# Two operand tiles swap roles behind a hybrid mixer, and four head groups are split beside the last projections

## The chip, the cores and the metric

The kernel runs on one core of one Trainium2 chip. The metric is the device time of one execution in microseconds, smaller is better. All 256 tokens of one sequence go through two transformer blocks in a single launch, everything in fp32. The large products use split operands: each fp32 matrix is written as hi + lo, both in the matmul format fp32r, and each product is the sum of hi·hi, lo·hi and hi·lo.

## The reference, cut to what matters

The model width is 2048. The first block is a conformer convolution and an MLP. The second block, in which the change lies, is

```python
x = x + hybrid_mixer(x, ...)      # below
x = x + cross_attention(x, mem, ...)
x = x + conv_ffn(x, ...)
return rmsnorm_2(x, final_norm_g)

def hybrid_mixer(x, ...):
    h = rmsnorm_2(x, norm_g)
    proj = h @ w_in                       # q, k, v, z (1024 each), b, a, then q, k, v of moba
    ...
    o_a = gated_delta_rule(l2norm(q_a), l2norm(k_a), v_a, g, beta)
    o_a = rmsnorm_2(o_a, gdn_norm_g) * silu(z_a)     # 8 heads of 128
    o_b = rmsnorm_2(moba_attention(q_b, k_b, v_b, rel_bias), moba_norm_g)   # 8 heads of 128
    return concatenate([o_a, o_b]) @ w_out           # 2048 x 2048
```

## The kernel before

**Weights.** Every weight matrix comes in slots of 512 KB. For a slot i, SP loads `w_raw`, ACT writes `w_hi` (L461), and DVE (L468) or POOL (L476), every other slot in the mixer, writes `w_lo`. Each of the three buffers is a ring of four. ACT makes `w_hi` of slot i+4 only when TensorE has used slot i.

**Order.** Every engine's program is written out by hand in the same order of slots. After each slot an engine calls `step()`, which advances the generators that are registered as work "beside" by one `yield` each. `finish()` steps until they are all over. An engine works strictly in its program's order, so a beside instruction that waits holds up the slots behind it.

**The mixer.** Counting slots from the mixer's first: six products `w_in` of 8 slots (1 to 48), six `moba` products (49 to 96), then z: `("w_in", 3, 0)` is slots 97 to 104 and `("w_in", 3, 1)` slots 105 to 112. Then comes `w_out`, eight pieces of 4 slots, 113 to 144, in `W_OUT_ORDER` = (1,0), (1,1), (0,0), (0,1), (1,2), (0,2), (1,3), (0,3). Half 1 contracts over the moba heads (parts 2 and 3 of the operand), half 0 over the delta-rule heads (parts 0 and 1); a part is four heads, 128 x 1024 values. Beside the slots runs `side_work`: both delta groups, moba heads 0 to 3, `norm(0)`, from step 98 on moba heads 4 to 7, `norm(1)` and, last, `gated(0)`. A moba head takes scores (L2061), bias and maximum on DVE (L2117 to L2124), exp on ACT (L2089), a turn by transposes (L2069), its copy on ACT (L2093), and the product with v (L2076). `norm(g)` scales rows on DVE (L2159), turns them on TensorE (L2031) and copies them back with a gain on ACT (L2038). `gated(g)` multiplies the delta output with silu(z) on DVE (L2372), then also L2031 and L2038. silu(z) is `z_block` (L2272), which reads the accumulator of `("w_in", 3, g)`.

**Operands.** `k.h` (`h_operand`, hi and lo, 16 tiles of 256 tokens) is the input of every `w_in` and `moba` product. The mixer's output is split into the same `k.h`, by `act_part` (hi, L649) and `dve_part` (lo, L655), so ACT first waits for the last `w_in` product:

```python
k.act_beside.finish()
act.wait_ge(*k.pe_done.at("w_in", 3, 1))
for g in range(2):
    act_part(k, act, k.h, 2 + g, CT, k.mk[g], k.act_done.at("moba norm", g), "heads_out")
```

TensorE runs `finish()`, in which the turn of `gated(0)` falls, between slot 112 and slot 113. `k.mid` (`mid_operand`) is the input of `xq` and of the FFN's gate and up products, and `k.h` then holds the cross-attention output and the FFN's hidden chunks. `k.mid` is allocated over the mixer's own work tiles, which are free by the time it is first written.

Of the kernel before, what the change touches and what calls it, by code (L numbers as in the profile page):

```python
# [229 lines left out]
class Kernel:  # L230
# [34 lines left out]
    def buffers(self):  # L265
# [38 lines left out]
        with ExitStack() as second:  # L304
            sb = lambda name, shape, dt=F32: self.sbuf(name, shape, dt, second)
            self.dt_bias, self.a_log = sb("dt_bias", [P, NG]), sb("a_log", [P, NG])
            self.beta, self.g, self.cum, self.grown, self.k_decay, self.beta_unit, self.beta_decay, self.half_log = (
                sb(n, [P, TT, NG]) for n in ("beta", "log_decay", "cum", "grown", "k_decay", "beta_unit", "beta_decay", "half_log"))
            self.logs, self.unit, self.o_small = (sb(n, [P, 2, TT, NG]) for n in ("logs", "unit", "o_small"))
            self.small = sb("gate_small", [P, 3, TT, NG])  # L310
            self.ba, self.token_col = sb("ba", [P, TT, 2 * NG]), sb("token_column", [P, TT])
            self.ba_rows = sb("ba_rows", [2 * NG, T])
            self.w_ba = sb("w_ba", [P, KT * 2 * NG])
            self.w_ba_hi, self.w_ba_lo = (sb(n, [P, KT * 2 * NG + P - 2 * NG], F32R) for n in ("w_ba_hi", "w_ba_lo"))
            self.work = sb("delta_work", [P, 5, TT, CT, P])
            self.state, self.ends = sb("state", [P, CT, HD]), sb("last_decay", [P, TT, 2, NG])
            self.pad = sb("conv_pad", [P, CT, GDN_K - 1 + T])
            self.v_own = sb("moba_v", [P, TT, NM * HD])
            self.moba_small, self.moba_root = sb("moba_small", [P, NM, 3, TT]), sb("moba_root", [P, NM, TT])
        self.mid = side_by_side(self.sbuf("mid_operand", [P, KT, 2, T], F32R))  # L320
# [1816 lines left out]
def act_moba_norm(k, act, g):  # L2137
    root = k.moba_root[:, g * CT:(g + 1) * CT, :]
    act.wait_ge(*k.dve_done.at("moba sums", g))
    act.activation(root, root, ACT.Ln, scale=1.0 / HD).then_inc(*k.act_done.mark())  # L2140
    act.wait_ge(*k.act_done.last())
    act.activation(root, root, ACT.Exp, scale=-0.5).then_inc(*k.act_done.mark("moba roots", g))
    yield
    act_turned(k, act, "moba norm", g, k.mk[g], "moba_norm_g_2")
    yield


def dve_moba_norm(k, dve, g):
# [12 lines left out]
    yield  # L2161

# [16 lines left out]

def side_work(delta, head, norm, gated):  # L2180
    steps = 0
# [13 lines left out]
    yield from counted(norm(1))  # L2195
    yield from counted(gated(0))


def pe_mixer(k, pe):
# [17 lines left out]
    k.pe_beside.start(after(3, pe_two_norms(k, pe)))  # L2217
    k.pe_beside.start(side_work(lambda g: pe_delta(k, pe, g), lambda h: pe_moba(k, pe, h), lambda g: pe_moba_norm(k, pe, g), gated))
    ready = operand_ready(k, "mix_norm")
# [9 lines left out]
    for g in range(2):  # L2229
        pe_product(k, pe, ("w_in", 3, g), k.h, ready, tokens_out=True)  # L2230
    k.pe_beside.finish()
    k.pe_beside.start(gated(1))
    heads_ready = operand_ready(k, "heads_out")
    for n, (half, b) in enumerate(W_OUT_ORDER):
        pe_product(k, pe, ("w_out", half, b), k.h, heads_ready, k_tiles=range(half * KT // 2, (half + 1) * KT // 2),
                   held=("mixer", b), opening=half == 1, closing=half == 0)


def act_mixer(k, act):
# [60 lines left out]
    k.act_beside.start(side_work(delta, lambda h: act_moba(k, act, h), lambda g: act_moba_norm(k, act, g), gated))  # L2300
    for g in range(2):
# [9 lines left out]
    for g in range(2):  # L2311
        act_product(k, act, ("w_in", 3, g), lambda: z_block(g))
    k.act_beside.finish()
    act.wait_ge(*k.pe_done.at("w_in", 3, 1))
    for g in range(2):
        act_part(k, act, k.h, 2 + g, CT, k.mk[g], k.act_done.at("moba norm", g), "heads_out")

    def first_half():
        yield
        act_part(k, act, k.h, 0, CT, k.z[0], k.act_done.at("gated", 0), "heads_out")  # L2320
        act_turned(k, act, "gated", 1, k.z[1], "gdn_norm_g_2")
        act_part(k, act, k.h, 1, CT, k.z[1], k.act_done.last(), "heads_out")
        yield
    k.act_beside.start(first_half())
    for half, b in W_OUT_ORDER:
        act_product(k, act, ("w_out", half, b),
                    None if half else (lambda: act_next(k, act, "xattn_norm", b, k.mid, None, ("w_out", 0, b), "xattn_norm_g_2")))


def dve_mixer(k, dve):  # L2330
# [39 lines left out]
    def gated(g):  # L2370
        dve.wait_ge(*k.act_done.at("z", g))
        dve.tensor_tensor(k.o[g], k.o[g], k.z_tok[g], ALU.mult).then_inc(*k.dve_done.mark("gated", g))  # L2372
        yield
        yield

    def add(b):
        dve_residual(k, dve, ("w_out", 0, b), b, ("mixer", b), [k.dve_done.at("group", "final1", b)])
        dve_prepare(k, dve, "xattn_norm", b, "xattn_norm_g_2", k.mid)
# [3 lines left out]
    k.dve_beside.start(side_work(lambda g: dve_delta(k, dve, g), lambda h: dve_moba(k, dve, h), lambda g: dve_moba_norm(k, dve, g),  # L2382
                                 gated))
    for g in range(2):
# [14 lines left out]
    def first_half():  # L2399
        yield  # L2400
        dve_part(k, dve, k.h, 0, CT, k.z[0], "heads_out")
        dve_part(k, dve, k.h, 1, CT, k.z[1], "heads_out")
        yield
    k.dve_beside.start(first_half())
    for half, b in W_OUT_ORDER:
# [25 lines left out]
def pe_cross(k, pe):  # L2431
    k.pe_beside.start(after(3, pe_total_beside(k, pe, "xattn_norm")))
    pe_product(k, pe, ("xq",), k.mid, operand_ready(k, "xattn_norm"))
    k.pe_beside.finish()
# [8 lines left out]
    for b in range(CT):  # L2443
        pe_product(k, pe, ("xo", b), k.h, operand_ready(k, "cross_out"), k_tiles=range(NX))


def act_cross(k, act):
# [11 lines left out]
    act.wait_ge(*k.pe_done.at("w_out", 0, CT - 1))  # L2459
    act_part(k, act, k.h, 0, NX, k.cross_o, k.act_done.last(), "cross_out")  # L2460
    for b in range(CT):
        act_product(k, act, ("xo", b), lambda: act_next(k, act, "ffn_norm", b, k.mid, ("xq",), ("xo", b), "ffn_norm_g_2"))


def dve_cross(k, dve):
# [11 lines left out]
    for _ in in_turn([head(h) for h in range(NX)], 3):  # L2477
        pass
    dve_part(k, dve, k.h, 0, NX, k.cross_o, "cross_out")

    def add(b):
        before = [k.act_done.at("squares", "xattn_norm", b)]
        dve_residual(k, dve, ("xo", b), b, ("xo", b), before)
        dve_prepare(k, dve, "ffn_norm", b, "ffn_norm_g_2", k.mid)
        k.dve_beside.start(after(1, dve_squares_of_x(k, dve, "ffn_norm", b)))
# [265 lines left out]
```

## Time and profile before

| | us |
|---|---|
| median of 3 runs | 2533.34 (2531.56 to 2536.05) |
| the profiled execution's own time | 2533.18 |
| its span, first to last instruction | 2531.9 |
| TensorE busy | 2449.0 (97%) |
| DVE / ACT / POOL busy | 1646.3 / 1119.0 / 258.9 |
| mean granted TensorE clock | 0.985 |

The span is what the trace covers, and the own time has 1.3 us around it. Times in the rows below are microseconds from the start of the span. In a timeline, the bracket at the end of a row is how long the engine sat idle before it and who released it. PE is TensorE.

### The profile page before, as it was taken

To read this page: it belongs to the slowest core of one execution; us is meant where nothing else is said; L and a number is where in the kernel's file an instruction comes from. 1 tells how busy PE (TensorE), PEld (TensorE's weight loads), DVE (VectorE), ACT (ScalarE), POOL (GpSimd) and SP (SyncE) were. 2 spreads that over 40 slices of the span, in tenths; PEclk is the share of its full clock that TensorE was granted. 3 is DMA by queue.
4 is the path that set the end of the run, shared out by engine and by line. 5 is a ranking of instruction groups with operands and counts; after the bars stand their busy time and mean duration, and the time that the engine had idled before them with its cause. 6 is when DMAs were issued, how large, how long until landed. Compare 5 with 4: busy or idle time off the path is not lost.

```text
span 2531.9 us, 36755 instructions
## 1 busy us (share of the span) xinstructions
PE 2449.0 (97%) x14956; PEld 2190.6 (87%) x14956; DVE 1646.3 (65%) x2274; ACT 1119.0 (44%) x1477; POOL 258.9 (10%) x129
## 2 busy tenths in 40 slices
PE   8999999999999999989899999897999999999997
PEld 7888698888888888889897998797888888888886
DVE  4999766666666666777646443354776676767677
ACT  4000445544454454455436355454544444444443
POOL 0000000000000000023323333330010000000000
PEclk9999999999999999999999999898999999999998
DMA  7445456665666666555334355352565655565663
GB/s 233 154 142 174 159 190 192 192 188 187 193 188 191 193 191 186 185 159 148 88 105 117 100 153 153 128 177 93 182 190 191 191 190 185 192 190 192 190 190 119
DMA packets 377575, 428.05 MB, mean 169 GB/s; under 512 B 16408, under 2 KB 323904, under 8 KB 377408
## 3 DMA queue, kind: packets, MB, share of 16 engines
q1 hardware_dynamic: 372288, 421.58, 54.0%
q10 hardware_dynamic: 5120, 4.12, 0.5%
q8 instruction: 120, 1.97, 0.3%
q14 instruction: 47, 0.39, 0.0%
HBM read 423.54 MB, written 3.67 MB: 169 GB/s over the span
## 4 chain that ended last, share of the span: by engine, by line
PE 92%; ACT 3%; DVE 3%; issue 1%; DMA 0%; POOL 0%; ACTq 0%; DVEq 0%
PE product L560 37%; PE product L509 19%; PE product L562 19%; PE product L534 10%; PE product L531 1%; ACT w_hi L461 1%; PE small L1675 1%; PE small L1689 1%; PE small L1685 1%; DVE w_lo L468 0%; DVE delta_work L1912 0%; DVE x_residual L617 0%; PE small L896 0%; PE small L1728 0%; DMA masks<-in_masks 0%
## 5 line engine op out<-in xcount | busy, mean ns | idle before, releaser
L468 DVE TENSOR_TENSOR w_lo<-w_raw,w_hi 128x1024 fp32r<-128x1024 f32 x640 | 794.1, 1244 | 533.9 <-ACT w_hi L461 533.1
L461 ACT ACTIVATE w_hi<-w_raw 128x1024 fp32r<-128x1024 f32 x712 | 750.4, 1057 | 861.7 <-PE product L562 568.7
L560 PE MATMUL product<-h_operand,w_hi 128*128 128x512 f32 x1728 | 600.0, 393 | 0.0
L560 PE MATMUL product<-mid_operand,w_hi 128*128 128x512 f32 x1408 | 490.2, 392 | 4.2 <-DVE x_residual L763 4.2
L562 PE MATMUL product<-h_operand,w_lo 128*128 128x256 f32 x1728 | 480.9, 278 | 0.0
L562 PE MATMUL product<-mid_operand,w_lo 128*128 128x256 f32 x1408 | 394.8, 280 | 0.0
L560 PEld LDWEIGHTS product<-h_operand,w_hi 128*128 128x128 f32 x1728 | 323.7, 187 | 73.6
L509 PE MATMUL product<-h_operand,w_hi 128*128 128x256 f32 x1920 | 361.3, 290 | 11.0 <-DVE h_operand L655 6.0
L560 PE MATMUL product<-mlp_hidden,w_hi 128*128 128x512 f32 x1024 | 355.7, 394 | 0.9 <-DVE x_residual L617 0.8
L476 POOL TENSOR_TENSOR w_lo<-w_raw,w_hi 128x1024 fp32r<-128x1024 f32 x72 | 180.7, 2510 | 1448.3 <-ACT w_hi L461 1448.3
L562 PEld LDWEIGHTS product<-h_operand,w_lo 128*128 128x128 f32 x1728 | 325.2, 188 | 0.0
L509 PEld LDWEIGHTS product<-h_operand,w_hi 128*128 128x128 f32 x1920 | 305.8, 196 | 15.5 <-POOL w_lo L476 4.0
L560 PEld LDWEIGHTS product<-mid_operand,w_hi 128*128 128x128 f32 x1408 | 264.1, 188 | 62.5 <-DVE x_residual L763 4.5
L562 PE MATMUL product<-mlp_hidden,w_lo 128*128 128x256 f32 x1024 | 283.7, 277 | 0.0
L509 PE MATMUL product<-h_operand,w_lo 128*128 128x256 f32 x960 | 274.7, 286 | 0.0
L562 PEld LDWEIGHTS product<-mid_operand,w_lo 128*128 128x128 f32 x1408 | 266.8, 189 | 0.0
L534 PE MATMUL product<-h_plain,w_raw 128*128 128x256 f32 x1024 | 224.2, 381 | 10.8 <-ACT h_plain L951 10.8
L560 PEld LDWEIGHTS product<-mlp_hidden,w_hi 128*128 128x128 f32 x1024 | 192.0, 188 | 46.2 <-DVE x_residual L617 1.1
L534 PEld LDWEIGHTS product<-h_plain,w_raw 128*128 128x128 f32 x1024 | 195.4, 191 | 38.1 <-DMA w_raw<-in_cc_w_in 10.8
L562 PEld LDWEIGHTS product<-mlp_hidden,w_lo 128*128 128x128 f32 x1024 | 192.1, 188 | 0.0
L1097 DVE SCALAR_TENSOR_TENSOR conv_out<-glu,feature_columns,conv_out 128x256 f32<-128x256 f32 x480 | 190.9, 478 | 0.0
L509 PEld LDWEIGHTS product<-h_operand,w_lo 128*128 128x128 f32 x960 | 187.5, 195 | 0.0
(291 smaller groups left out, 2277.0 us busy)
## 6 DMA issues: line engine op xcount, KB each, us to landing
w_raw<-in_mlp_w SPq DMA_DIRECT2D x256, 512.0 KB, 3.7
w_raw<-in_w_in SPq DMA_DIRECT2D x112, 512.0 KB, 3.8
w_raw<-in_w_gate SPq DMA_DIRECT2D x88, 512.0 KB, 3.5
w_raw<-in_w_up SPq DMA_DIRECT2D x88, 512.0 KB, 3.8
w_raw<-in_w_down SPq DMA_DIRECT2D x88, 512.0 KB, 3.4
w_raw<-in_cc_w_in SPq DMA_DIRECT2D x128, 256.0 KB, 3.0
w_raw<-in_cc_w_out SPq DMA_DIRECT2D x32, 512.0 KB, 4.6
w_raw<-in_w_out SPq DMA_DIRECT2D x32, 512.0 KB, 4.2
```

Source lines behind the costliest of these rows:

```text
L461: act.activation(k.w_hi[i % SPLIT], k.w_raw[i % RAW], ACT.Copy).then_inc(*k.act_done.mark("w_hi", i))
L468: dve.tensor_tensor(k.w_lo[i % SPLIT], k.w_raw[i % RAW], k.w_hi[i % SPLIT].bitcast(F32), ALU.subtract).then_inc(*k.dve_done.mark("w_lo", i))
L476: pool.tensor_tensor(k.w_lo[i % SPLIT], k.w_raw[i % RAW], k.w_hi[i % SPLIT].bitcast(F32), ALU.subtract).then_inc(*k.pool_done.mark("w_lo", i))
L509: done = pe.matmul(out, stationary, moving, start=first and opens, stop=final, skip_group_check=True)
L531: done = pe.matmul(psum[:, part * COLS:(part + 1) * COLS], x[:, kt, cut(part)], w[:, kk, :], start=first, stop=final, skip_group_check=True)
L534: done = pe.matmul(psum[:, part * T:(part + 1) * T], w[:, kk, cut(part)], x[:, kt, :], start=first and part % 2 == 0, stop=final, skip_gro ...
L560: pe.matmul(out, hi[:, kk, n], x.both[:, kt].rearrange("p a t -> p (a t)"), start=s == 0 and kk == 0, stop=False, skip_group_check=True)
L562: done = pe.matmul(out[:, 0:T], lo[:, kk, n], x.hi[:, kt, :], start=False, stop=last and kk == WIDE_K - 1, skip_group_check=True)
L1097: dve.scalar_tensor_tensor(out=out, in0=tap, scalar=w, in1=out, op0=ALU.mult, op1=ALU.add).then_inc(*k.dve_done.mark("tap", t, b, j))
L1675: done = pe.matmul(bank[:, cut(h)], k.off[t][:, h, :], k.a[t][:, h, :], start=True, stop=True)
L1685: done = pe.matmul(bank[:, cut(h)], u[:, h, :], y[:, h, :], start=True, stop=True)
L1689: done = pe.matmul(bank[:, cut(h)], y[:, h, :], u[:, h, :], start=True, stop=True)
```

## The change

The mixer's output is split into `k.mid` in place of `k.h`. `k.h` becomes the operand that `k.mid` was (input of `xq`, gate and up), and `k.mid` takes over the cross-attention output and the FFN's hidden chunks. The tile `mid_operand` is allocated higher up (a spacer `below_mid`), over the parts of the mixer's work tiles that are free early, and these tiles are reordered. With that, the splits need no longer wait for the last `w_in` product: parts 2 and 3 are split inside `norm(0)` and `norm(1)`, part 0 and part 1 inside `gated(0)` and `gated(1)`. `gated(0)` leaves `side_work` and is started after `("w_in", 3, 0)`, beside `("w_in", 3, 1)`; `gated(1)` is started after the `finish()` behind `("w_in", 3, 1)`.

```diff
+            below_mid = 2 * NG + 8 * TT * NG + 3 * 2 * TT * NG + 3 * TT * NG + TT * 2 * NG + TT + NM * 3 * TT + NM * TT + TT * NM * HD
+            self.work = sb("delta_work", [P, 5, TT, CT, P])
...
+        self.sbuf("below_mid", [P, below_mid + TT * CT * P])
         self.mid = side_by_side(self.sbuf("mid_operand", [P, KT, 2, T], F32R))
...
-        self.ffn_mid = [side_by_side(self.h.both[:, i * CT:(i + 1) * CT]) for i in range(FFN_MID)]
+        self.ffn_mid = [side_by_side(self.mid.both[:, i * CT:(i + 1) * CT]) for i in range(FFN_MID)]
@@ act_moba_norm
     act_turned(k, act, "moba norm", g, k.mk[g], "moba_norm_g_2")
+    act_part(k, act, k.mid, 2 + g, CT, k.mk[g], k.act_done.at("moba norm", g), "heads_out")
     yield
@@ dve_moba_norm
     yield
+    dve_part(k, dve, k.mid, 2 + g, CT, k.mk[g], "heads_out")
     yield
@@ side_work
     yield from counted(norm(1))
-    yield from counted(gated(0))
@@ pe_mixer
     for g in range(2):
         pe_product(k, pe, ("w_in", 3, g), k.h, ready, tokens_out=True)
-    k.pe_beside.finish()
-    k.pe_beside.start(gated(1))
+        if g:
+            k.pe_beside.finish()
+        k.pe_beside.start(gated(g))
...
-        pe_product(k, pe, ("w_out", half, b), k.h, heads_ready, ...
+        pe_product(k, pe, ("w_out", half, b), k.mid, heads_ready, ...
@@ act_mixer
     def gated(g):
         yield
         act_turned(k, act, "gated", g, k.z[g], "gdn_norm_g_2")
+        act_part(k, act, k.mid, g, CT, k.z[g], k.act_done.last(), "heads_out")
         yield
...
         act_product(k, act, ("w_in", 3, g), lambda: z_block(g))
-    k.act_beside.finish()
-    act.wait_ge(*k.pe_done.at("w_in", 3, 1))
-    for g in range(2):
-        act_part(k, act, k.h, 2 + g, CT, k.mk[g], k.act_done.at("moba norm", g), "heads_out")
-
-    def first_half():
...
-    k.act_beside.start(first_half())
+        if g:
+            k.act_beside.finish()
+        k.act_beside.start(gated(g))
@@ dve_mixer
         dve.tensor_tensor(k.o[g], k.o[g], k.z_tok[g], ALU.mult).then_inc(*k.dve_done.mark("gated", g))
         yield
         yield
+        dve_part(k, dve, k.mid, g, CT, k.z[g], "heads_out")
+        yield
...
-    k.dve_beside.finish()
-    for _ in gated(1):
-        pass
-    for g in range(2):
-        dve_part(k, dve, k.h, 2 + g, CT, k.mk[g], "heads_out")
...
```

In cross-attention and the FFN only the names `k.h` and `k.mid` swap.

## Rows read from the trace of the kernel before

**Rows 1.** The page, busy time and the chain that ended last, by engine.

```profile
PE 2449.0 (97%) x14956; PEld 2190.6 (87%) x14956; DVE 1646.3 (65%) x2274; ACT 1119.0 (44%) x1477; POOL 258.9 (10%) x129
...
PE 92%; ACT 3%; DVE 3%; issue 1%; DMA 0%; POOL 0%; ACTq 0%; DVEq 0%
```

**Rows 2.** Timeline of all engines, from the end of slot 112 to slot 113.

```profile
1594.74 0.40 PE L509 MATMUL product<-w_lo,h_operand 128*128 128x512 f32 x1
1595.17 1.27 ACT L2272 ACTIVATE heads<-product,token_column 128x512 f32<-128x512 f32 x2 [2.20 <-PE product L509]
1596.33 1.05 ACT L461 ACTIVATE w_hi<-w_raw 128x1024 fp32r<-128x1024 f32 x1
1597.42 1.23 DVE L468 TENSOR_TENSOR w_lo<-w_raw,w_hi 128x1024 fp32r<-128x1024 f32 x1 [7.82 <-ACT w_hi L461]
1598.56 2.35 DVE L2372 TENSOR_TENSOR heads<-heads 128x1024 f32<-128x1024 f32 x2
...
1599.93 1.94 PE L2031 MATMUL small<-masks,heads 128*128 128x128 f32 x8 [4.79 <-DVE heads L2372]
...
1602.49 1.99 ACT L649 ACTIVATE h_operand<-heads 128x1024 fp32r<-128x1024 f32 x2
1603.57 2.36 DVE L655 TENSOR_TENSOR h_operand<-heads,h_operand 128x1024 fp32r<-128x1024 f32 x2 [2.65 <-ACT h_operand L649]
...
1604.94 0.77 PE L509 MATMUL product<-h_operand,w_hi 128*128 128x256 f32 x2 [3.07 <-DVE h_operand L655]
```

**Rows 3.** Busy time, granted clock (PEclk) and DMA share of these stretches.

```profile
1590.90:1594.20 3.30, 3.30 (x9) 2.59 (x8) 0.00 (x0) 2.05 (x3) 0.92 (x1) 0.50 0.31 101
...
1604.90:1607.80 2.90, 2.86 (x13) 2.89 (x14) 1.03 (x1) 0.00 (x0) 0.00 (x0) 0.50 0.00 0
1607.80:1609.40 1.60, 1.60 (x15) 1.60 (x14) 0.00 (x0) 0.00 (x0) 0.00 (x0) 0.98 0.00 0
```

**Rows 4.** Timeline of ACT from slot 113 on.

```profile
1609.44 1.06 ACT L461 ACTIVATE w_hi<-w_raw 128x1024 fp32r<-128x1024 f32 x1 [4.96 <-PE product L509]
...
1621.83 1.06 ACT L461 ACTIVATE w_hi<-w_raw 128x1024 fp32r<-128x1024 f32 x1 [1.82 <-PE product L509]
1624.71 1.06 ACT L461 ACTIVATE w_hi<-w_raw 128x1024 fp32r<-128x1024 f32 x1 [1.82 <-PE product L509]
```

**Rows 5.** Timeline of ACT and DVE, slots 104 to 108.

```profile
1564.10 1.27 ACT L2272 ACTIVATE heads<-product,token_column 128x512 f32<-128x512 f32 x2 [0.17 <-PE product L509]
...
1568.79 0.17 DVE L2124 TENSOR_SCALAR moba_small<-moba_small 128x2 f32<-128x2 f32 x1
...
1570.93 1.06 ACT L461 ACTIVATE w_hi<-w_raw 128x1024 fp32r<-128x1024 f32 x1 [1.66 <-PE product L509]
...
1574.11 0.19 ACT L2089 ACTIVATION_READ_ACCUMULATOR delta_work<-delta_work,moba_small 128x1 f32 x1
1574.20 1.04 ACT L461 ACTIVATE w_hi<-w_raw 128x1024 fp32r<-128x1024 f32 x1
...
1574.44 0.52 PE L2069 MATMUL small<-masks,delta_work 128*128 128x128 f32 x3 [0.88 <-ACT delta_work L2089]
...
1575.15 0.47 ACT L2093 ACTIVATE delta_work<-small 128x384 f32<-128x384 f32 x1
```

**Rows 6.** The chain in order of time: start, us, what. Head 7's last step; a turn at full clock.

```profile
1577.74 0.67 PE small L2076 x6
...
1612.23 0.87 PE small L2031 x8
```

**Rows 7.** Timeline of ACT and DVE around norm(0), steps 91 to 96.

```profile
1531.36 0.69 ACT L2038 ACTIVATE heads<-small,feature_columns 128x512 f32<-128x512 f32 x1 [0.17 <-PE small L2031]
1534.97 1.06 ACT L461 ACTIVATE w_hi<-w_raw 128x1024 fp32r<-128x1024 f32 x1 [2.93 <-PE product L509]
...
1537.80 1.22 DVE L752 TENSOR_TENSOR heads<-product,rows 128x1024 f32<-128x1024 f32 x1 [7.42 <-PE product L509]
```

**Rows 8.** Timeline around norm(1), steps 110 to 112.

```profile
1589.74 1.06 PE L2031 MATMUL small<-masks,heads 128*128 128x128 f32 x8 [3.14 <-DVE heads L2159]
1590.40 1.27 ACT L2038 ACTIVATE heads<-small,feature_columns 128x512 f32<-128x512 f32 x2 [1.12 <-PE small L2031]
...
1591.69 1.28 ACT L2272 ACT_TABLE_LOAD   x1
```

**Rows 9.** The page's costliest groups, products that read h_operand and mid_operand.

```profile
L560 PE MATMUL product<-h_operand,w_hi 128*128 128x512 f32 x1728 | 600.0, 393 | 0.0
L560 PE MATMUL product<-mid_operand,w_hi 128*128 128x512 f32 x1408 | 490.2, 392 | 4.2 <-DVE x_residual L763 4.2
L562 PE MATMUL product<-h_operand,w_lo 128*128 128x256 f32 x1728 | 480.9, 278 | 0.0
L562 PE MATMUL product<-mid_operand,w_lo 128*128 128x256 f32 x1408 | 394.8, 280 | 0.0
```

More of the change, by code:

```diff
@@ L314, in buffers @@
             self.w_ba_hi, self.w_ba_lo = (sb(n, [P, KT * 2 * NG + P - 2 * NG], F32R) for n in ("w_ba_hi", "w_ba_lo"))
[L315 to L319, printed above, removed]
+        self.sbuf("below_mid", [P, below_mid + TT * CT * P])
         self.mid = side_by_side(self.sbuf("mid_operand", [P, KT, 2, T], F32R))
@@ L2177, with side_work @@
 SECOND_HEADS_AT = 97
-def side_work(delta, head, norm, gated):
+def side_work(delta, head, norm):
     steps = 0
@@ L2217, in pe_mixer @@
     k.pe_beside.start(after(3, pe_two_norms(k, pe)))
-    k.pe_beside.start(side_work(lambda g: pe_delta(k, pe, g), lambda h: pe_moba(k, pe, h), lambda g: pe_moba_norm(k, pe, g), gated))
+    k.pe_beside.start(side_work(lambda g: pe_delta(k, pe, g), lambda h: pe_moba(k, pe, h), lambda g: pe_moba_norm(k, pe, g)))
     ready = operand_ready(k, "mix_norm")
@@ L2230, in pe_mixer @@
         pe_product(k, pe, ("w_in", 3, g), k.h, ready, tokens_out=True)
-    k.pe_beside.finish()
-    k.pe_beside.start(gated(1))
+        if g:
+            k.pe_beside.finish()
+        k.pe_beside.start(gated(g))
     heads_ready = operand_ready(k, "heads_out")
     for n, (half, b) in enumerate(W_OUT_ORDER):
-        pe_product(k, pe, ("w_out", half, b), k.h, heads_ready, k_tiles=range(half * KT // 2, (half + 1) * KT // 2),
+        pe_product(k, pe, ("w_out", half, b), k.mid, heads_ready, k_tiles=range(half * KT // 2, (half + 1) * KT // 2),
                    held=("mixer", b), opening=half == 1, closing=half == 0)
@@ L2296, in gated @@
         act_turned(k, act, "gated", g, k.z[g], "gdn_norm_g_2")
+        act_part(k, act, k.mid, g, CT, k.z[g], k.act_done.last(), "heads_out")
         yield
     k.act_beside.start(after(3, start()))
-    k.act_beside.start(side_work(delta, lambda h: act_moba(k, act, h), lambda g: act_moba_norm(k, act, g), gated))
+    k.act_beside.start(side_work(delta, lambda h: act_moba(k, act, h), lambda g: act_moba_norm(k, act, g)))
     for g in range(2):
@@ L2312, in act_mixer @@
         act_product(k, act, ("w_in", 3, g), lambda: z_block(g))
-    k.act_beside.finish()
-    act.wait_ge(*k.pe_done.at("w_in", 3, 1))
-    for g in range(2):
-        act_part(k, act, k.h, 2 + g, CT, k.mk[g], k.act_done.at("moba norm", g), "heads_out")
-    def first_half():
[L2319 to L2323, printed above, removed]
-    k.act_beside.start(first_half())
+        if g:
+            k.act_beside.finish()
+        k.act_beside.start(gated(g))
     for half, b in W_OUT_ORDER:
         act_product(k, act, ("w_out", half, b),
-                    None if half else (lambda: act_next(k, act, "xattn_norm", b, k.mid, None, ("w_out", 0, b), "xattn_norm_g_2")))
+                    None if half else (lambda: act_next(k, act, "xattn_norm", b, k.h, ("w_in", 3, 1), ("w_out", 0, b), "xattn_norm_g_2")))
 def dve_mixer(k, dve):
@@ L2374, in gated @@
         yield
+        dve_part(k, dve, k.mid, g, CT, k.z[g], "heads_out")
+        yield
     def add(b):
         dve_residual(k, dve, ("w_out", 0, b), b, ("mixer", b), [k.dve_done.at("group", "final1", b)])
-        dve_prepare(k, dve, "xattn_norm", b, "xattn_norm_g_2", k.mid)
+        dve_prepare(k, dve, "xattn_norm", b, "xattn_norm_g_2", k.h)
         k.dve_beside.start(after(1, dve_squares_of_x(k, dve, "xattn_norm", b)))
     k.dve_beside.start(after(3, start()))
-    k.dve_beside.start(side_work(lambda g: dve_delta(k, dve, g), lambda h: dve_moba(k, dve, h), lambda g: dve_moba_norm(k, dve, g),
-                                 gated))
+    k.dve_beside.start(side_work(lambda g: dve_delta(k, dve, g), lambda h: dve_moba(k, dve, h), lambda g: dve_moba_norm(k, dve, g)))
     for g in range(2):
@@ L2392, in dve_mixer @@
         dve_product(k, dve, ("w_in", 3, g))
-    k.dve_beside.finish()
-    for _ in gated(1):
-        pass
-    for g in range(2):
-        dve_part(k, dve, k.h, 2 + g, CT, k.mk[g], "heads_out")
[L2399 to L2404, printed above, removed]
+        if g:
+            k.dve_beside.finish()
+        k.dve_beside.start(gated(g))
     for half, b in W_OUT_ORDER:
@@ L2432, in pe_cross @@
     k.pe_beside.start(after(3, pe_total_beside(k, pe, "xattn_norm")))
-    pe_product(k, pe, ("xq",), k.mid, operand_ready(k, "xattn_norm"))
+    pe_product(k, pe, ("xq",), k.h, operand_ready(k, "xattn_norm"))
     k.pe_beside.finish()
@@ L2443, in pe_cross @@
     for b in range(CT):
-        pe_product(k, pe, ("xo", b), k.h, operand_ready(k, "cross_out"), k_tiles=range(NX))
+        pe_product(k, pe, ("xo", b), k.mid, operand_ready(k, "cross_out"), k_tiles=range(NX))
 def act_cross(k, act):
@@ L2459, in act_cross @@
     act.wait_ge(*k.pe_done.at("w_out", 0, CT - 1))
-    act_part(k, act, k.h, 0, NX, k.cross_o, k.act_done.last(), "cross_out")
+    act_part(k, act, k.mid, 0, NX, k.cross_o, k.act_done.last(), "cross_out")
     for b in range(CT):
-        act_product(k, act, ("xo", b), lambda: act_next(k, act, "ffn_norm", b, k.mid, ("xq",), ("xo", b), "ffn_norm_g_2"))
+        act_product(k, act, ("xo", b), lambda: act_next(k, act, "ffn_norm", b, k.h, ("xq",), ("xo", b), "ffn_norm_g_2"))
 def dve_cross(k, dve):
@@ L2478, in dve_cross @@
         pass
-    dve_part(k, dve, k.h, 0, NX, k.cross_o, "cross_out")
+    dve_part(k, dve, k.mid, 0, NX, k.cross_o, "cross_out")
     def add(b):
@@ L2497, in pe_ffn @@
                 k.pe_beside.start(after(3, pe_total_beside(k, pe, "ffn_norm")))
-            pe_wide_product(k, pe, ("gate", c), k.mid, operand_ready(k, "ffn_norm"))
-            pe_wide_product(k, pe, ("up", c), k.mid, operand_ready(k, "ffn_norm"))
+            pe_wide_product(k, pe, ("gate", c), k.h, operand_ready(k, "ffn_norm"))
+            pe_wide_product(k, pe, ("up", c), k.h, operand_ready(k, "ffn_norm"))
         else:
-            hidden = side_by_side(k.h.both[:, (2 * c % FFN_MID) * CT:(2 * c % FFN_MID + 2) * CT])
+            hidden = side_by_side(k.mid.both[:, (2 * c % FFN_MID) * CT:(2 * c % FFN_MID + 2) * CT])
             for b in range(CT):
```

6 lines of the change are left out of this document (5 added, 1 removed).

## The prediction

> **What bounds the kernel now.** I read the page first: TensorE is busy for 97% of the span and holds 92% of the chain that ended last [rows 1]. So a microsecond counts only if it is one in which TensorE stands still or runs slowly. The chain of waits, asked for TensorE alone, then gives two idle times of TensorE at the seam between `w_in` and `w_out`, and the timeline shows what fills them [rows 2]. The last matmul of slot 112 ends at 1595.14. Then `finish()` reaches the turn of `gated(0)`, which wants the gated product of DVE, and DVE's L2372 is queued behind `w_lo` of slot 116, which waits for `w_hi`, which stands behind `z_block(1)` on ACT: z 1.27, w_hi 1.05, w_lo 1.23, multiply, in one line. TensorE waits 4.79 us. The turn takes 1.94 us, twice the 0.87 of the same eight transposes later [rows 6]. Then TensorE waits 3.07 us for the first hi and lo of the moba heads, which wait for the turn's copies and for the end of slot 112. Slot 113 starts at 1604.94.
>
> The windows show a second loss. TensorE's granted clock is 0.50 (1.2 GHz) up to 1607.8 and 0.98 and 1.00 (2.4 GHz) after that [rows 3]; what preceded the low level is a stretch of nearly 10 us with only eight transposes in it. The `w_hi` behind slot 113 starts at 1609.44, 4.50 us after slot 113 began, while later slots of the same size follow each other every 2.88 us (1621.83 to 1624.71) [rows 4]. Before each of these ACT was idle until TensorE released it, so ACT and the loads are ahead of TensorE there.
>
> **The change part by part.** Durations are from the one profiled execution, whose own time is 2533.18 us, 0.16 below the median 2533.34; the sum is made against it.
>
> *Removed at the seam.* The 4.79 us wait, the 1.94 us turn and the 3.07 us wait: 9.80 us between 1595.14 and 1604.94. After slot 112 nothing is left in `finish()` for TensorE. Slot 113 needs parts 2, `w_lo` 113 (made 4 slots earlier) and an accumulator, the one that `z_block(0)` emptied at 1565.37 [rows 5]. Slot 115 is the first that reads part 3.
>
> *The clock behind it.* Slot 113 took 4.50 less the 0.08 that ACT needs to start, 4.42 us; at full clock 2.88. That gives back 1.54 us. By the Trainium skill (TensorE: Matmul & The Clock Gate, "What's actually happening"), the half rate is the default and sustained activity releases it, and the moment at which the level changes varies from run to run. The trace agrees with the first: 0.50 behind the idle stretch. By the second the 1.54 us would not be the same in each run; no run here shows that.
>
> *gated(0), moved beside slots 105 to 107.* z(0) is there at 1565.37. On DVE the multiply comes behind head 7's maximum, which ends at 1568.96 [rows 5]; with 1.22 us it is done at 1570.2. TensorE reaches step 106 at about 1570.87 (the `w_hi` that this releases starts at 1570.93), so it doesn't wait: a margin of 0.65 us. The turn costs 0.87 us at full clock there. But in the step behind, TensorE waits 0.88 us for head 7's exp [rows 5], and that wait shrinks by what the turn takes. Net nothing; without that cover 0.87.
>
> *ACT's share of it.* The two copies (1.27 us) and hi of part 0 (1.05 us) come behind exp, which ends at 1574.30, and in front of `w_hi` of slot 111, and that in front of head 7's turned copy L2093. In a row, with the 0.1 by which ACT's instructions overlap: w_hi at 1576.5, L2093 at 1577.5, done at 1577.95, with 0.14 of signalling 1578.1. TensorE wants it at 1577.74 [rows 6]. About 0.4 us of new wait; I take 0.5, from 0 (if TensorE comes later) to 2.3 (all of ACT's added work). Who waits behind it: `w_hi` 111 goes from 1574.20 to 1576.5, POOL's `w_lo` takes 2.4 us, ready before 1580, and TensorE uses slot 111 at about 1584. The later `w_hi` are released by TensorE again. DVE's lo of part 0 waits for hi in front of `w_lo` 112, which ACT makes only after that.
>
> *norm(0) with part 2.* ACT sat idle for 2.93 us before 1534.97, hi takes 1.05; DVE had 7.42 us idle before 1537.80, lo takes 1.23 [rows 7]. Nothing.
>
> *norm(1) with part 3.* TensorE's 3.14 us wait for L2159 stays, as does the low clock behind it (0.50 from 1590.90 to 1594.20 [rows 3]). ACT's hi comes behind the copies, from 1591.65 to 1592.7, in front of the table load for silu (1.28 us) [rows 8]. So z(1) is ready to start at 1594.0 plus the 0.5 from above, and slot 112 ends at 1595.14 or later: hidden by 0.6 us or more. If it is not, `w_hi` 116 is later, for which slot 116 leaves 8 us. DVE was idle for 7.82 us before 1597.42 [rows 2]: lo of part 3 is free there.
>
> *gated(1) with part 1.* DVE multiplies behind `w_lo` 116, done by 1600. TensorE turns at step 114, after 5.76 us of `w_out`, about 1601.4. hi and lo follow by 1606. Part 0 and part 1 are read from slots 121 and 123 on, 20 us later. As before, the turn costs TensorE 0.87 us, so no difference.
>
> *The swapped tiles.* The number of splits and copies is the same, no load is added and SP's order of loads stays. `act_next` for `xattn_norm` waits for `("w_in", 3, 1)`, long past. The products that read h_operand and mid_operand last the same within 2 ns (393 and 392, 278 and 280) [rows 9]: nothing for the new places; by these rows the bounds are 1408 × 2 ns, 2.8 us, either way, but the durations overlap, so less.
>
> Sum: 9.80 + 1.54 − 0.5 = 10.8 us. 2533.18 − 10.8 = 2522.4. Everything behind the seam is ordered by TensorE's slots and moves up as a block.
>
> **The rivals.**
>
> *The full gain (forecast), 74%.* 2522.4, own range 2520.0 to 2525.5. The upper end is the ACT bound (1.8 more) and the turn uncovered (0.87); the lower end is the tile bound or a milder low clock at norm(1), which costs 3.30/2 = 1.65 us now.
>
> *Part is given back beside slots 105 to 112, 14%.* ACT has exp, copies, hi, w_hi and L2093 in one line, and the DVE margin is only 0.65 us. If TensorE idles long enough there to fall to the low clock again, as it did behind 3.14 us at norm(1), it pays up to 2.3 for the wait, 0.87 for the turn and 1.65 for the clock, 4.8 in all instead of 0.5: 10.8 − 4.3 = 6.5, so 2526.7 (2525.5 to 2528.3). Against it: each item's cover is read from rows.
>
> *The weight supply takes over, 6%: no change.* If `w_hi`, `w_lo` and loads needed the pause at the seam to get ahead, the slots of `w_out` would come at the supply's pace, and the time would stay near 2533. It would have to cost 10.8 us over the 32 slots, 0.34 us on each 2.88. Against it: ACT's idle 1.82 us before each `w_hi` [rows 4].
>
> *The tile's new place slows the products, 6%: slower.* h_operand and mid_operand change roles for the 1408 pairs of matmuls of gate and up, and the hidden chunks too. It decides when a pair (392 + 280 ns) takes 10.8/1408 = 7.7 ns more, 1.1%; at 2% it is 18.9 us against 10.8, hence 2541. Against it: rows 9 differ by 2 ns [rows 9] though these tiles lie in different places already.
>
> **How the numbers follow.** A measurement of this kernel tells about 0.2% (5.1 us) from no change, so faster means below 2528.3. Forecast and partial loss lie there: 0.88. Supply: 0.06 the same. Place: 0.06 slower. The range for 8 in 10 takes the forecast's whole range and the nearer part of the partial case: 2520.0 to 2527.0.
>
> **What would show it.** In the profile of the changed kernel, TensorE's waits for L2372 and for the split of the heads are gone, and the first `w_out` matmul stands directly behind slot 112 at a clock of 1.00. The turn of `gated(0)` lies between slots 106 and 107 and takes about 0.9 us; the wait for exp is about 0; a new wait of about 0.5 us for L2093 stands in front of L2076. The 3.1 us wait at norm(1) is still there. Wrong would be: a wait of TensorE for `w_lo` in slots 107 to 120, a low clock in the first `w_out` slots, or matmuls of gate and up that differ by more than 2 ns.

## The result, and the profile after

The changed kernel takes 2521.25 us (median of 4 runs, 2520.34 to 2524.37), the kernel before in the same runs 2532.45 (2531.12 to 2536.05): 11.2 us less, ratio 0.995 with an interval of [0.9938, 0.9961]. Forecast were 10.8 us less, 2522.4. The profiled execution took 2520.34 us with a span of 2519.0.

Below are lines of the list of TensorE's waits in the changed kernel, longest total first; "us in total, times, longest us". Most line numbers are two to four higher than before; DVE's gated product, L2372 before, is L2368.

```profile
PE product L536 <- ACT h_plain L953: 10.0, 1, 10.0
...
PE small L2033 <- DVE heads L2162: 5.9, 2, 3.1
...
PE product L562 <- DVE x_residual L765: 4.7, 1, 4.7
...
PE small L2078 <- DVE mid_operand L657: 0.2, 1, 0.2
```

The 4.79 us for the gated product and the 3.07 us for hi and lo of the moba heads [rows 2] have gone from it. The turn of norm(0) and norm(1) waits as before (5.9 in all), and one short wait is new. The timeline of TensorE shows the seam:

```profile
1570.70 1.03 PE L2033 MATMUL small<-masks,heads 128*128 128x128 f32 x8
1574.47 0.52 PE L2071 MATMUL small<-masks,delta_work 128*128 128x128 f32 x3
1577.99 0.91 PE L2078 MATMUL small<-moba_v,delta_work 128*128 128x128 f32 x6 [0.23 <-DVE mid_operand L657]
...
1590.23 1.06 PE L2033 MATMUL small<-masks,heads 128*128 128x128 f32 x8 [3.14 <-DVE heads L2162]
...
1595.24 0.39 PE L511 MATMUL product<-w_lo,h_operand 128*128 128x512 f32 x1
1595.47 0.40 PE L511 MATMUL product<-mid_operand,w_hi 128*128 128x256 f32 x2
...
1601.08 1.04 PE L2033 MATMUL small<-masks,heads 128*128 128x128 f32 x8
```

The first row is gated(0)'s turn at step 106, at full clock and without a wait. Head 7's turn (L2071) starts at 1574.47, before it was 1574.44 [rows 5], and no longer shows a wait in front of it: the turn of gated(0) fills the time in which TensorE waited for exp. Slot 113 starts 0.23 us after the last matmul of slot 112 started. gated(1)'s turn, at 1612.07 before and two slots behind the seam, starts at 1601.08: 11.0 us earlier.

The windows of the same execution (us, then busy time of TensorE, its weight loads, DVE, ACT and POOL, then granted clock, DMA share, GB/s):

```profile
1590.90:1594.20 3.30, 3.30 (x12) 2.62 (x11) 0.92 (x1) 3.25 (x4) 1.41 (x1) 0.55 0.15 50
1595.50:1604.00 8.50, 8.50 (x75) 8.50 (x74) 3.59 (x3) 5.91 (x8) 2.85 (x1) 1.00 0.22 70
```

The low clock behind norm(1)'s wait is there as before (0.50, now 0.55 [rows 3]); in `w_out`'s first slots it is 1.00 where it was 0.50.

ACT and DVE took over the moved work as reckoned:

```profile
1574.23 1.24 ACT L2040 ACTIVATE heads<-small,feature_columns 128x512 f32<-128x512 f32 x2
1575.51 1.06 ACT L651 ACTIVATE mid_operand<-heads 128x1024 fp32r<-128x1024 f32 x1
1576.47 1.04 ACT L463 ACTIVATE w_hi<-w_raw 128x1024 fp32r<-128x1024 f32 x1
1577.42 0.47 ACT L2095 ACTIVATE delta_work<-small 128x384 f32<-128x384 f32 x1
...
1592.19 1.06 ACT L651 ACTIVATE mid_operand<-heads 128x1024 fp32r<-128x1024 f32 x1
1593.27 1.28 ACT L2276 ACT_TABLE_LOAD   x1
1595.67 1.27 ACT L2276 ACTIVATE heads<-product,token_column 128x512 f32<-128x512 f32 x2 [1.12 <-PE product L511]
```

L2095, head 7's copy, stood at 1577.5 in the prediction and starts at 1577.42; it started at 1575.15 before [rows 5]. The table load in front of z(1) ends at 1594.55, 1.12 us before TensorE releases the copy.

One thing was not in the prediction. From gated(1)'s turn on, ACT's `w_hi` follow each other every 2.80 us, not every 2.88 as before [rows 4]:

```profile
1616.22 1.06 ACT L463 ACTIVATE w_hi<-w_raw 128x1024 fp32r<-128x1024 f32 x1 [1.74 <-PE product L511]
1619.02 1.06 ACT L463 ACTIVATE w_hi<-w_raw 128x1024 fp32r<-128x1024 f32 x1 [1.74 <-PE product L511]
```

TensorE releases both, so its 24 matmuls of a slot take 117 ns each in place of 120. In the chain that ended last, the 816 matmuls from gated(1)'s turn on take 2.4 us less; the kernel before, then the changed one:

```profile
1613.10 97.91 PE product L509 x816
```

```profile
1602.11 95.52 PE product L511 x816
```

With this the profiled pair (12.8 us apart in own time) is a little further apart than the medians.

### The profile page after: what moved, and what is told of

Same layout as the page of the kernel before. It is cut to its first block, busy times and chain, and to the rows that moved or that the text cites. A ratio compares the mean times of both kernels' runs of the same rounds, so it can differ in the third digit from the quotient of the medians.

```text
span 2519.0 us, 36758 instructions
## 1 busy us (share of the span) xinstructions
PE 2447.4 (97%) x14956; PEld 2189.5 (87%) x14956; DVE 1647.1 (65%) x2274; ACT 1119.0 (44%) x1477; POOL 260.3 (10%) x129
## 4 chain that ended last, share of the span: by engine, by line
PE 93%; DVE 3%; ACT 3%; issue 1%; DMA 0%; POOL 0%; ACTq 0%; DVEq 0%
PE product L562 37%; PE product L511 20%; PE product L564 19%; PE product L536 10%; PE product L533 1%; ACT w_hi L463 1%; PE small L1677 1%; PE small L1691 1%; PE small L1687 1%; DVE delta_work L1914 0%; DVE w_lo L470 0%; DVE x_residual L619 0%; PE small L1634 0%; PE small L898 0%; PE small L1730 0%
## 5 line engine op out<-in xcount | busy, mean ns | idle before, releaser
L562 PE MATMUL product<-h_operand,w_hi 128*128 128x512 f32 x2432 | 846.0, 393 | 4.7 <-DVE x_residual L765 4.7
L564 PE MATMUL product<-h_operand,w_lo 128*128 128x256 f32 x2432 | 677.5, 279 | 0.0
L562 PEld LDWEIGHTS product<-h_operand,w_hi 128*128 128x128 f32 x2432 | 456.2, 188 | 108.7 <-DVE x_residual L765 5.0
L564 PEld LDWEIGHTS product<-h_operand,w_lo 128*128 128x128 f32 x2432 | 458.5, 189 | 0.1
L511 PE MATMUL product<-h_operand,w_hi 128*128 128x256 f32 x1408 | 266.7, 291 | 5.0 <-POOL w_lo L478 3.3
L562 PE MATMUL product<-mid_operand,w_hi 128*128 128x512 f32 x704 | 244.3, 390 | 0.0
L511 PEld LDWEIGHTS product<-h_operand,w_hi 128*128 128x128 f32 x1408 | 223.8, 195 | 8.4 <-POOL w_lo L478 3.9
L511 PE MATMUL product<-h_operand,w_lo 128*128 128x256 f32 x704 | 201.4, 286 | 0.0
L564 PE MATMUL product<-mid_operand,w_lo 128*128 128x256 f32 x704 | 198.5, 282 | 0.0
L619 DVE TENSOR_TENSOR x_residual<-x_residual,product 128x512 f32<-128x512 f32 x224 | 153.7, 686 | 40.4 <-PE product L564 36.3
L562 PEld LDWEIGHTS product<-mid_operand,w_hi 128*128 128x128 f32 x704 | 132.1, 188 | 27.8
L511 PEld LDWEIGHTS product<-h_operand,w_lo 128*128 128x128 f32 x704 | 137.5, 195 | 0.0
```

What stands on the lines that cost most here:

```text
L511: done = pe.matmul(out, stationary, moving, start=first and opens, stop=final, skip_group_check=True)
L562: pe.matmul(out, hi[:, kk, n], x.both[:, kt].rearrange("p a t -> p (a t)"), start=s == 0 and kk == 0, stop=False, skip_group_check=True)
L564: done = pe.matmul(out[:, 0:T], lo[:, kk, n], x.hi[:, kt, :], start=False, stop=last and kk == WIDE_K - 1, skip_group_check=True)
L619: dve.tensor_tensor(x, x, row, ALU.add).then_inc(*k.dve_done.mark("added", *key, half))
```

## The experiments

Two numbers are used beside the times. The **stretch** is the time from the start of head 7's product with v (the last `L2078` or, in the kernel before, `L2076` in TensorE's timeline) to the start of the sum for `xattn_norm` behind `w_out` (L708, L706): 133.3 us before (1577.58 to 1710.85), 119.5 after (1577.99 to 1697.47). It holds the seam and all of `w_out` and leaves out what varies elsewhere. The **slot** is the distance of ACT's `w_hi` in `w_out`.

**1. The roles and places alone (swap_only).** The operand names and the allocation of the changed kernel, the mixer's schedule of the kernel before (the edit is shown against the kernel before, cut to the mixer):

```diff
@@ act_mixer, against the kernel before
     act.wait_ge(*k.pe_done.at("w_in", 3, 1))
     for g in range(2):
-        act_part(k, act, k.h, 2 + g, CT, k.mk[g], k.act_done.at("moba norm", g), "heads_out")
+        act_part(k, act, k.mid, 2 + g, CT, k.mk[g], k.act_done.at("moba norm", g), "heads_out")
@@ pe_mixer
-        pe_product(k, pe, ("w_out", half, b), k.h, heads_ready, ...
+        pe_product(k, pe, ("w_out", half, b), k.mid, heads_ready, ...
```

> The roles and places of the two operand tiles as in the changed kernel, the schedule as in the kernel before: the splits of the mixer's output wait for the last w_in product, gated(0) is last in the side work. Theory 1 (the schedule brings the gain at the seam, about 10.8 us, and the new place of mid_operand a little more, because w_out's matmuls follow each other every 117 ns in place of 120): TensorE's waits of 4.8 and 3.1 us are back with the low clock behind them, the pace of w_out is 117 ns, 2.4 us less than before, so 2530. Theory 2 (the place is nothing, the pace differed by chance): the pace is 120 ns, time equal to before, 2532.5. Theory 3 (the place brings most of it): clearly below 2528.

Measured: 2530.49 us (2527.78 to 2536.50, 10 runs) against 2535.35 for before in the same runs, ratio 0.9981 [0.9971, 0.9990]. Stretch 130.1 us, slot 2.80. TensorE's timeline and its chain (start, us, what):

```profile
1589.63 1.07 PE L2033 MATMUL small<-masks,heads 128*128 128x128 f32 x8 [3.14 <-DVE heads L2161]
1598.23 1.94 PE L2033 MATMUL small<-masks,heads 128*128 128x128 f32 x8 [4.79 <-DVE heads L2374]
```

```profile
1603.24 0.77 PE L511 MATMUL product<-mid_operand,w_hi 128*128 128x256 f32 x2 [3.07 <-DVE mid_operand L657]
```

```profile
1590.70 2.77 PE product L511 x12
...
1603.24 8.10 PE product L511 x48
```

Both seam waits are back to the hundredth (4.79 and 3.07), and the pace of `w_out` stays at 117 ns. So theory 1 holds: from gated(1)'s turn to the end of the stretch it takes 96.4 us, as in the changed kernel, against 98.8 before, so the place brings 2.4; the schedule brings the seam's share, 130.1 to 119.5 in the stretch. The times agree: 4.9 us less than before, and run 3, whose splits lie beside the slots, is another 9.5 below this one in the same runs. In this execution the low clock lay elsewhere. Slot 112 ran at full clock (2.77 us in the chain, against 4.35 before) although the same 3.14 us of idle stood in front of it, which is 1.6 less; slots 113 and 114 together took 8.10 us against 7.29, 0.8 more, for the clock stayed low longer there. That is why the stretch is another 0.8 us shorter than 133.3 − 2.4.

**2. gated(0) last in the side work again (gated0_last).**

```diff
     yield from counted(norm(1))
+    yield from counted(gated(0))
...
-        if g:
-            k.pe_beside.finish()
-        k.pe_beside.start(gated(g))
+    k.pe_beside.finish()
+    k.pe_beside.start(gated(1))
```

> The changed kernel, but gated(0) last in the side work again, so that its turn falls between slot 112 and slot 113; the moba heads are still split beside. If the two waits at the seam are independent, as the prediction's sum took them: the 4.8 us wait for the gated product is back, the 3.1 us wait for hi and lo of the moba heads is not; the low clock lasts from the turn on for some 4.5 us. Against before: 3.07 us for the wait, nearly nothing for the clock, 2.4 for w_out's pace, so 5.5 us less than before, 2527. If the split at the seam was only in the shadow of the gated chain, both waits go or both come: 2521 or 2530.

Measured: 2525.68 us (2523.13 to 2533.03, 9 runs), ratio 0.9967 [0.9957, 0.9977]; stretch 127.3 us, slot 2.80.

```profile
1600.90 1.94 PE L2033 MATMUL small<-masks,heads 128*128 128x128 f32 x8 [4.79 <-DVE heads L2367]
```

The 4.79 us wait is back, the one for the heads' hi and lo is not. The stretch of before, less 2.4 for the pace and 3.07 for the wait, is 127.8. The two waits are separate terms, as the sum took them. In the medians the run lies 9.7 us below the kernel before (interval 5.8 to 10.9), where 5.5 was expected and the stretch shows 6.0; the rows don't explain the surplus of the medians.

**3. hi and lo of part 0 one step later (hi_next_step).**

```diff
         act_turned(k, act, "gated", g, k.z[g], "gdn_norm_g_2")
+        yield
-        act_part(k, act, k.mid, g, CT, k.z[g], k.act_done.last(), "heads_out")
+        act_part(k, act, k.mid, g, CT, k.z[g], k.act_done.at("gated", g), "heads_out")
```

> The changed kernel, with hi and lo of part 0 one step later, so that on ACT they stand behind w_hi of slot 111 and head 7's turned copy. The 0.25 us that TensorE waits in front of head 7's last product goes if ACT's copy (L2095, ended 1577.89) is what it waits for: 0.3 us less, not to be told from the changed kernel in the time, but seen in the profile. If DVE's lo of part 0 is the releaser, as the profile names it, the wait goes as well only because that moves too; then ACT's copy would have been early. The time: 2521, same as the changed kernel.

Measured: 2521.01 us (2520.00 to 2525.99), ratio 0.9948 [0.9932, 0.9964], stretch 119.4: the same as the changed kernel. The wait in front of head 7's product with v is gone:

```profile
1574.80 0.52 PE L2071 MATMUL small<-masks,delta_work 128*128 128x128 f32 x3
1577.93 0.83 PE L2078 MATMUL small<-moba_v,delta_work 128*128 128x128 f32 x6
```

From head 7's turn to this product it takes 3.13 us, against 3.52 in the changed kernel, so the later start cost 0.4 us, of which the profile shows 0.23 as idle. Moving hi and lo of part 0 made it go. In the program, this product waits for ACT's copy and not for DVE, yet the profile names DVE's split, which ended at 1577.83, next to the copy's 1577.89. The run moved both and doesn't separate them.

**4. The turns of norm(0) and norm(1) one step later (norm_turn_later)**, on the changed kernel:

```diff
 def pe_moba_norm(k, pe, g):
     yield
+    yield
     pe_turn(...)
@@ act_moba_norm, behind "moba roots", and dve_moba_norm, behind "moba normed"
     yield
+    yield
```

> The changed kernel, with the turns of norm(0) and norm(1) (and the copies and splits behind them) one step later on TensorE, ACT and DVE, so that a slot of matmuls covers DVE's L2162. Expected: the waits of 2.7 and 3.1 us shrink to 0.0 to 0.5, the low clock behind them (0.50 for 3.3 us behind norm(1), the turn at half speed behind norm(0)) goes: 2.4 + 0.8 and 2.8 + 1.6, so 7 to 8 us less than the changed kernel, 2514. Rival: the work that moves behind slot 112 (z, w_hi, copies, hi in one line on ACT) makes lo of part 3 late for slot 115, and 2 to 4 us of it come back as a wait of TensorE for L657: 2517.

Measured: 2517.86 us (2516.68 to 2518.36), ratio 0.9931 [0.9916, 0.9946]: 3.4 us less than the changed kernel, half of what was expected. The two waits are gone but for 0.4 us; another came at gated(1)'s turn:

```profile
PE small L2033 <- DVE heads L2371: 3.3, 1, 3.3
PE small L2033 <- DVE heads L2164: 0.4, 1, 0.4
PE small L2078 <- DVE mid_operand L657: 0.2, 1, 0.2
```

The part at norm(0) paid: from head 0's scores to head 7's last product TensorE takes 91.05 us in place of 95.47. The part at norm(1) did not: the stretch is 120.2 us against 119.5. The rival had part of the mechanism (more work in one line behind slot 112) and the wrong place: lo of part 3 was in time, what was late was DVE's product for gated(1) behind it.

```profile
1594.55 1.22 DVE L657 TENSOR_TENSOR mid_operand<-heads,mid_operand 128x1024 fp32r<-128x1024 f32 x1 [1.03 <-ACT mid_operand L651]
1595.69 3.37 DVE L2371 TENSOR_TENSOR heads<-heads 128x1024 f32<-128x1024 f32 x1
```

```profile
1595.54 2.43 POOL L478 TENSOR_TENSOR w_lo<-w_raw,w_hi 128x1024 fp32r<-128x1024 f32 x1 [4.26 <-ACT w_hi L463]
```

Most of this wait is the multiply itself. It took 3.37 us here, in run 5 too, and 1.22 us in the changed kernel; POOL's subtraction had begun 0.15 us before it. With 1.22 it would have ended 2.15 us earlier, so by this estimate the longer line behind slot 112 alone accounts for some 1.2 us of the 3.3.

**5. Both 3 and 4 (both).**

> The turns of norm(0) and norm(1) one step later and hi and lo of part 0 one step later, on the changed kernel. Sum of the two: about 8 us less than the changed kernel, 2513.5. Rival: gated(0)'s turn at step 106 shifts against head 7, and the waits for exp and for the turned copy come in another place: 2514 to 2516.

Measured: 2517.12 us (2514.06 to 2518.74), ratio 0.9933 [0.9916, 0.9950], stretch 120.2. Both values expected, 2513.5 and 2514 to 2516, were missed. As in the fourth run, a wait (3.4 us) stands at gated(1)'s turn. The sum that was expected left that wait out.

**6. The turn of gated(1) two steps later as well (all_turns_later)**, on the fourth:

```diff
-        k.pe_beside.start(gated(g))
+        k.pe_beside.start(after(2 * g, gated(g)))
@@ the same in act_mixer; in dve_mixer the product keeps its step:
+        yield from idle(2 * g)
         dve_part(k, dve, k.mid, g, CT, k.z[g], "heads_out")
```

> The run with the turns of norm(0) and norm(1) one step later, and in addition the turn, copies and splits of gated(1) two steps later, behind slot 116, since in that run TensorE waited 3.3 us in front of gated(1)'s turn for DVE's product of z(1) and had a clock of 0.65 behind it. Part 1 is wanted only by slot 123. Expected: the wait of 3.3 us goes and the turn takes 0.9 in place of 1.9 us, slots behind it at full clock: 4 to 5 us less than that run, 8 less than the changed kernel, 2513. Rival: DVE's product stays late for another step and 1 to 3 us of wait remain: 2515.

> The changed kernel once more, on the chip of the run with all turns later, as its yardstick; and the pace of w_out's slots: 2.80 us if the tile's place sets it (as in the seven runs with this place so far), 2.80 or 2.88 by chance if the run does, as for the convolution's output product, which shows 2.81 or 2.88 at one and the same place.

Measured on one and the same chip: 2517.71 us (2510.38 to 2518.45), ratio 0.9923 [0.9904, 0.9942], and for the changed kernel again (after_again) 2522.95 (2519.40 to 2524.19), ratio 0.9950 [0.9935, 0.9965]. The waits between step 90 and the end of `w_out` are down to 0.6 us, and the stretch is 115.5 us, 4.7 less than in run 4. DVE's multiply is as slow as there (3.42 us), but now nothing waits for it. The two windows together, 91.04 and 115.51, are 8.4 us less than in the changed kernel's first profile (95.47 and 119.48). The medians show 5.2 of them. The granted clock over 1700 to 1800 us, where nothing was changed, was 0.85 in this profile and 0.93 in that of run 4, and its span (2516.5) is that of run 4 (2516.4): in the profiled execution what the stretch gained was lost behind it. The 2513 that was expected was not reached, nor is the median clearly below run 4's. The interval also overlaps slightly with the changed kernel's, so this gain is shown in the rows (8.4 us) and only roughly in the time (5.2 us between medians).

**7. The place of mid_operand (mid_minus_32, mid_minus_64, h_plus_32, and three kernels repeated).** One number changes, the spacer below `mid_operand`, by 8 or 16 values of 4 bytes; in h_plus_32 a spacer of 8 values stands below `h_operand` and shifts all tiles from there on.

```diff
-        self.sbuf("below_mid", [P, below_mid + TT * CT * P])
+        self.sbuf("below_mid", [P, below_mid + TT * CT * P - 8])
```

> The changed kernel with mid_operand 32 bytes lower. It starts at an odd multiple of 32 bytes in the changed kernel (behind 3464 values of 4 bytes), at a multiple of 64 in the kernel before. If the start modulo 64 bytes sets the pace of the 256-column matmuls: w_out goes back from 117 to 120 ns, 2.4 us more than the changed kernel, 2523.6. If the region counts: 117 ns stays, 2521.

> The changed kernel with mid_operand 64 bytes lower, again at an odd multiple of 32. By the theory of the start modulo 64: 117 ns, 2521. By the theory of a distance to another tile in small steps: another pace than in the run with 32 bytes and than in the changed kernel.

> The changed kernel with a spacer of 32 bytes below h_operand, which moves h_operand and all tiles above it, weights and mid_operand included. If the operand's own start modulo 64 sets the pace: the w_in, moba and xq matmuls of 256 columns go from 120 to 117 ns, w_out back to 120: w_in's six products and four moba products are 10 x 8 x 24 = 1920 matmuls, and xq and others 192, so some 6 us less, w_out 2.4 more, in all about 3 to 4 less than the changed kernel. If the offset between the operand and the weights counts: h against the weights is as before, mid against the weights too, nothing changes, 2521.

> The kernel before once more, one look. If the operand's place sets w_out's pace, its slots follow every 2.88 us again; if it is a chance of the run, 2.80 may show.

> mid_operand 32 bytes lower once more, one look. By the place: 2.88 us a slot again. By chance: 2.80 as likely.

| | time, us | slot in w_out, us | stretch, us | slot in cc_out, us |
|---|---|---|---|---|
| before | 2532.45 | 2.88 | 133.3 | 2.88 |
| before_again | 2536.62, one run | 2.88 | 134.6 | 2.81 |
| changed kernel | 2521.25 | 2.80 | 119.5 | 2.88 |
| after_again | 2522.95 | 2.80 | 117.9 | 2.81 |
| mid_minus_32 | 2522.17 | 2.88 | 122.0 | 2.88 |
| mid_minus_32_again | 2522.59, one run | 2.88 | 120.5 | 2.81 |
| mid_minus_64 | 2523.61 | 2.84 | 120.8 | 2.81 |
| h_plus_32 | 2521.08 | 2.80 | 119.5 | 2.88 |

ACT's rows of mid_minus_32, then of mid_minus_64:

```profile
1620.30 1.06 ACT L463 ACTIVATE w_hi<-w_raw 128x1024 fp32r<-128x1024 f32 x1 [1.82 <-PE product L511]
1623.18 1.06 ACT L463 ACTIVATE w_hi<-w_raw 128x1024 fp32r<-128x1024 f32 x1 [1.82 <-PE product L511]
```

```profile
1621.05 1.06 ACT L463 ACTIVATE w_hi<-w_raw 128x1024 fp32r<-128x1024 f32 x1 [1.78 <-PE product L511]
1623.89 1.06 ACT L463 ACTIVATE w_hi<-w_raw 128x1024 fp32r<-128x1024 f32 x1 [1.78 <-PE product L511]
```

32 bytes lower, the slots take 2.88 us in both profiles; 64 bytes lower, 2.84 in its one profile; in all nine profiles with the changed kernel's place, the shifted h_plus_32 among them, 2.80. So the place sets the pace of `w_out`, and it is worth 2.4 us in the stretch. The theory of the start modulo 64 bytes is refuted twice: 64 lower is not like the changed kernel, and h_plus_32 moves the start of mid_operand by 32 bytes without any effect, and `xq` on the shifted h_operand still takes 11.52 us for 96 matmuls. In h_plus_32 the weight tiles move along with the operand. That fits a distance between operand and weights, but no run shifted the weights alone, so it stays open what the pace hangs on. The times hardly tell these kernels apart: their intervals overlap, though all four runs of mid_minus_64 lie above all four of h_plus_32.

The profile of mid_minus_64 shows a second difference. From its first wide matmul on, the FFN takes 754.6 us; in the thirteen other profiles it takes 749.6 to 750.0. The surplus lies in the 704 pairs of the down product, which read mid_operand; the changed kernel, then mid_minus_64:

```profile
L562 PE MATMUL product<-mid_operand,w_hi 128*128 128x512 f32 x704 | 244.3, 390 | 0.0
```

```profile
L562 PE MATMUL product<-mid_operand,w_hi 128*128 128x512 f32 x704 | 248.9, 397 | 0.0
```

So a place can slow the 512-column products too. Only one profile shows it, and the median of mid_minus_64 is 2.4 us above the changed kernel's, not the 6 that this and the slots would add up to.

The last column is a product that no edit touches (`cc_out`, 311 to 392 us, 672 matmuls in 80.90 or 78.92 us). Its pace is 2.88 or 2.81 us a slot at one and the same place, in different executions. So about 2 us of difference between executions come from there, and why is open. The changed kernel, then the same kernel again:

```profile
310.76 80.90 PE product L511 x672
```

```profile
310.86 78.92 PE product L511 x672
```

## Why the prediction was right at the seam and wrong about the tile

The time, 2521.25 us, lies in the stated range, and the mechanism forecast for the seam is what the rows show. The step that failed is the term for the swapped tiles, "nothing for the new places": `w_out` runs at 117 ns a matmul in place of 120, and that is worth 2.4 us. That the medians still differ by 11.2 us, next to the forecast 10.8, is in part luck: the profiled pair, in which every term can be read, is 12.9 us apart in span.

**The seam.** The 9.80 us of idle time and turn are gone. The clock term was too large. The prediction took slot 113 as 4.42 us from the start of ACT's `w_hi`; in TensorE's timeline of the kernel before slot 114 starts at 1609.18, 4.24 us after slot 113, so the low clock cost 1.36 us there, not 1.54. The new place hid this, for it gives 2 × 0.08 us more in slots 113 and 114. gated(1)'s turn starts 11.0 us earlier: 9.80 + 1.36 + 0.16, another 0.16 because slot 112 ran a little faster, less 0.49 by which norm(1)'s turn starts later. Run 1 puts the two seam waits down to the schedule, and run 2 takes the wait for the gated product and that for the heads' hi and lo apart.

```profile
1609.18 0.40 PE L509 MATMUL product<-h_operand,w_hi 128*128 128x256 f32 x2
```

**gated(0) beside slots 105 to 107.** There was no wait for DVE's product, and the turn, inside the former wait for exp, cost nothing. The new wait was reckoned at 0.4 and taken as 0.5. The profile shows 0.23 us of idle, but from head 7's turn to its product with v it takes 3.52 us where it took 3.14, so the cost is the 0.4 that was reckoned. The instructions on ACT came where they were reckoned; the copy ended at 1577.89 and not at 1577.95.

**norm(0), norm(1), gated(1).** Free, as forecast, and the waits of norm(0) and norm(1) stayed as they were. Runs 4 and 6 show that the first really was a loss of 4.4 us, and that the second only pays when gated(1) makes room.

**The tile's place.** The prediction took nothing, from durations of the FFN's pairs of matmuls [rows 9], and set a rival on the other side. Those rows compare the two old places; nothing read an operand at the new one, so no row of before could show what it does. The bound of 2.8 us was counted over gate and up only, and the 768 matmuls of `w_out` were left out of it. The FFN indeed didn't change: from its first wide matmul to the end of the span 749.85 us before (1782.05 to 2531.9) and 749.82 after (1769.18 to 2519.0). But `w_out` did, by 2.4 us to the good. That the error lay within the range is luck, since the bound was worked out for other products.

**The spread.** Of the profiled pair's difference of 12.9 us in span, 11.0 lie at the seam and 2.4 behind it in `w_out`, and 0.5 went the other way after that. The medians are 11.2 apart. The 1.7 us between the two are within what one kernel's executions differ by (2531.1 to 2536.1, 2520.3 to 2524.4): the convolution's two paces are worth 2.0 and slot 112's low clock 1.6. By the Trainium skill (TensorE: Matmul & The Clock Gate, "What's actually happening") the moment at which the level changes varies from run to run. The trace agrees: behind the same 3.14 us of idle slot 112 took 2.77 us in run 1 and 4.19 in run 2.

## What to carry to other kernels

When the bounding engine runs dry between two phases, write down what the first instruction of the next phase waits for, link by link: here a shared buffer forced splits, which were ready long before, to wait for the last reader, and a small turn at the end of the side work pulled a chain of four instructions on two engines into the gap. Give the output a buffer of its own and start each small piece as soon as its input is there. Then look at once for what the same engines do in line next: in run 4 a covered wait of 3.1 us only came back as 3.3 us two steps further, in part because a multiply there ran beside POOL and took 3.37 us instead of 1.22, until that step had room too. And when a change moves an operand, count every product that reads it at its new place, and leave a term with bounds for its pace: rows of other places say nothing about it.

## What the runs showed of the hardware that was not expected

- The start of an operand tile, in steps of 32 bytes, goes with the pace of 256-column matmuls on it in `w_out`: 117 and 120 ns (slots of 2.80 and 2.88 us), repeated in nine and two profiles, and 118 ns (2.84) in one. The 512-column products were slower at one of the four places only, 64 bytes lower, by 4.6 us in 704, in one profile.
- The same product, at the same place, runs at 117.4 or 120.4 ns a matmul in different executions (78.92 or 80.90 us for 672).
- The same multiply of 128x1024 took 1.22 us on DVE at 1568.88 of the changed kernel and 3.37 us in run 4, where POOL had started a subtraction of the same size 0.15 us before it (1595.54, 2.43 us long); runs 5 and 6 show the same (3.37 and 3.42). In the changed kernel, where the multiply began first, POOL's subtraction at 1569.38 took 2.97 us in place of 2.40. That the two engines hold each other up fits these rows but was not tested.
